# A GLA scan stage in which output buffers alternate through all heads, loads stand between the stores, and turned keys are copied behind the square

## What is computed

```python
g_f = (log_sigmoid(r_f @ w_af + b_af) / GATE_NORM).reshape(B, T, N_HEADS_GLA, HEAD_DK)
...
o_f, s_f = _gla_scan(q, k, v, g_f, s_f0)
o_b, s_b = _gla_scan(q[:, ::-1], k[:, ::-1], v[:, ::-1], g_b[:, ::-1], s_b0)
o = (o_f + o_b[:, ::-1]).astype(x.dtype)
o = _rmsnorm(o, gla_norm_g).reshape(B, T, GLA_VDIM) * jax.nn.silu(gate_a)
```

## Time and profile before

| | |
|---|---|
| median of 3 runs | 2041.45 us (2041.24 to 2043.97) |
| the profiled execution, its own time | 2043.08 us |
| its span in the trace | 2041.3 us |
| PE busy | 1946.9 us (95%) |
| PE weight loads | 1779.2 us (87%) |
| DVE busy | 997.1 us (49%) |
| ACT busy | 889.3 us (44%) |
| POOL busy | 576.2 us (28%) |
| mean granted TensorE clock | 0.982 |

### The profile page before, as it was taken

The page is one execution under the profiler, slowest core; times in us unless marked ns, Lnnn a source line. Parts: engine busy times, 40 slices in busy tenths (PEclk is TensorE's granted clock), DMA queues, the critical chain, the costliest instruction groups (busy, mean ns, idle before and its releaser), DMA issues.

```text
span 2041.3 us, 30175 instructions
## 1 busy us (share of the span) xinstructions
PE 1946.9 (95%) x10585; PEld 1779.2 (87%) x10585; DVE 997.1 (49%) x1854; ACT 889.3 (44%) x1905; POOL 576.2 (28%) x643
## 2 busy tenths in 40 slices
PE   7899999999999999999999988779899999999997
PEld 2899999999999999999999776667798888898886
DVE  4778887764444345444443244445566422333333
ACT  3565667744445574344553245556643100211222
POOL 0236652323433314333330000000931022331122
PEclk9899999999999999999999998889899999999999
DMA  6578888777878887778889583552356666654433
GB/s 272 199 261 300 282 283 320 285 253 226 283 262 274 292 292 237 243 259 267 280 273 350 187 332 141 204 217 86 123 217 226 216 213 210 228 194 169 143 123 124
DMA packets 165243, 476.90 MB, mean 234 GB/s; under 512 B 14512, under 2 KB 51818, under 8 KB 156396
## 3 DMA queue, kind: packets, MB, share of 16 engines
q1 hardware_dynamic: 151276, 424.70, 60.4%
q10 hardware_dynamic: 13824, 50.34, 6.2%
HBM read 310.34 MB, written 155.20 MB: 228 GB/s over the span
## 4 chain that ended last, share of the span: by engine, by line
PE 85%; DMA 6%; DVE 3%; ACT 2%; POOL 2%; issue 1%; SPq 1%; POOLq 0%; ACTq 0%; DVEq 0%
PE bank L2020 48%; PE bank L2319 10%; PE bank L2271 10%; PE bank L2284 5%; PE bank L2148 2%; DMA og_dram<-og 2%; PE bank L2213 1%; PE bank L2137 1%; DMA w_raw<-in_w_in 1%; PE bank L2115 1%; POOL h_lo L970 1%; DMA v_ld<-v_dram 1%; PE bank L2044 1%; DMA x_st<-in_x 1%; PE bank L2060 1%
## 5 line engine op out<-in xcount | busy, mean ns | idle before, releaser
L2020 PE MATMUL bank<-h_hi,w_op 128*128 128x384 f32 x4032 | 1054.7, 337 | 11.2 <-DVE h_lo L1517 6.0
L2020 PEld LDWEIGHTS bank<-h_hi,w_op 128*128 128x128 f32 x4032 | 732.2, 188 | 15.1 <-issue 15.1
L2020 PE MATMUL bank<-h_lo,w_op 128*128 128x384 f32 x2016 | 675.1, 335 | 0.0
L2020 PEld LDWEIGHTS bank<-h_lo,w_op 128*128 128x128 f32 x2016 | 379.8, 188 | 0.0
L1511 DVE TENSOR_TENSOR w_op<-w_raw,w_op 128x512 fp32r<-128x512 f32 x240 | 187.3, 781 | 126.2 <-ACT w_op L1143 122.4
L1143 ACT ACTIVATE w_op<-w_raw 128x512 fp32r<-128x512 f32 x240 | 150.2, 627 | 161.6 <-PE bank L2020 154.1
L995 POOL TENSOR_TENSOR decs<-decs,qk_s 128x192 f32<-128x192 f32 x192 | 122.1, 672 | 333.7 <-ACT decs L1217 333.5
L2319 PE MATMUL bank<-in_a,pwa 128*128 128x512 f32 (+1 forms) x960 | 197.3, 368 | 0.0
L2319 PEld LDWEIGHTS bank<-in_a,pwa 128*128 128x128 f32 x960 | 167.3, 189 | 30.0
L2271 PE MATMUL bank<-ow,me_hi 128*128 128x512 f32 x576 | 177.3, 389 | 0.0
L1566 DVE TENSOR_TENSOR outs<-bank,u 128x384 f32<-128x384 f32 x180 | 99.5, 553 | 118.8 <-PE bank L2020 117.9
(11 more groups left out here) (222 smaller groups left out, 2647.4 us busy)
## 6 DMA issues: line engine op xcount, KB each, us to landing
w_op<-wt_dram SPq DMA_DIRECT2D x192, 512.0 KB, 5.4
wt_dram<-w_op ACTq DMA_DIRECT2D x96, 512.0 KB, 4.4
w_raw<-in_w_in SPq DMA_DIRECT2D x48, 768.0 KB, 5.9
w_raw<-in_w_in SPq DMA_DIRECT2D x24, 1024.0 KB, 6.8
qk_dec<-decs SPq DMA_DIRECT2D x48, 384.0 KB, 6.6
mg_dram<-outs SPq DMA_DIRECT2D x24, 768.0 KB, 6.8
swap<-qk_s SPq DMA_DIRECT2D x48, 192.0 KB, 5.6
v_dram<-outs SPq DMA_DIRECT2D x24, 384.0 KB, 4.8
```

Source lines behind the costliest of these rows:

```text
L2020: ins = pe.matmul(bnk, w_op[slot][:, part, k, :], h[:, j, k, :], start=(first and k == 0 and part == 0 and h is h_hi), stop=(k == HK - 1 a ...
```

## The change

The edits, all in the scan stage:

1. `og` buffers are chosen by the running number of the block, `NB * head + b`, modulo 2; the waits of `gate` and the last waits of SP are counted to match.
2. `load_keys` no longer loads the queries. `load_queries(head + 1)` is issued behind the store of block 0, `load_gates(head + 1)` behind that of block 1, `load_first_values(head + 2)` behind that of block 2. The parts of u are loaded in two pairs, one ahead of and one behind the store of block 4 of head 2.
3. On ACT, the first `k_out` of a step (of term run + 1) is issued one step earlier, between the square and the Ln.

```diff
--- before.py
+++ after.py
@@ -748,12 +748,14 @@
                 else:
                     load_values(head, 0, LT - V_FIRST)
                     load_values(head, LT, NT)
-                load_queries(head)
 
             def load_queries(head):
                 n, d = head % 2, kept_way(head)
                 sp.dma_start(kk[n][:, 1 - d, :], qk_dec[4 + head, :, 1 - d]).then_inc(s_ql[n], 16)
                 sp.dma_start(qd[n][:, :, :], qk_dec[head]).then_inc(s_ql[n], 16)
+
+            def load_mixed(g):
+                sp.dma_start(uf[:, g, :], u_dram[g]).then_inc(s_big[g], 16)
 
             def load_gates(head):
                 sp.dma_start(ga_ld[head % 2][:, :, :], ga_dram[2 * head:2 * head + 2].rearrange("e p n -> p e n")
@@ -773,28 +775,31 @@
             sp.wait_ge(s_ql[0], 32)
             load_keys(1)
             load_first_values(1)
-            load_gates(1)
             sp.wait_ge(s_pu, NKEPT)
             store_state(0, kept_way(0))
             for head in range(HEADS):
                 for b in range(NB):
                     t0, n = head_tokens(head, b)
-                    if b == 3 and head + 2 < HEADS:
-                        sp.wait_ge(s_o, NT * head + V_FIRST)
-                        load_first_values(head + 2)
                     if b == NB - 1 and head + 2 <= HEADS:
                         sp.wait_ge(s_o, NT * head + NT)
                         if head + 2 < HEADS:
                             load_keys(head + 2)
                         else:
-                            for g in range(GROUPS):
-                                sp.dma_start(uf[:, g, :], u_dram[g]).then_inc(s_big[g], 16)
+                            load_mixed(0)
+                            load_mixed(1)
                     sp.wait_ge(s_gt, NT * head + BLOCKS[b][0] // P + n // P)
                     sp.dma_start(og_dram[2 * head:2 * head + 2, :, t0:t0 + n].rearrange("e p n -> p e n"),
-                                 og[:, b % 2, :, 0:n]).then_inc(s_ogst[b % 2], 16)
-                if head + 2 < HEADS:
-                    load_gates(head + 2)
-                elif head + 2 == HEADS:
+                                 og[:, (NB * head + b) % 2, :, 0:n]).then_inc(s_ogst[(NB * head + b) % 2], 16)
+                    if b == 0 and head + 1 < HEADS:
+                        load_queries(head + 1)
+                    if b == 1 and head + 1 < HEADS:
+                        load_gates(head + 1)
+                    if b == 2 and head + 2 < HEADS:
+                        sp.wait_ge(s_o, NT * head + V_FIRST)
+                        load_first_values(head + 2)
+                if head + 2 == HEADS:
+                    load_mixed(2)
+                    load_mixed(3)
                     sp.dma_start(tab_e_raw[:, :, :, :], io["tab_e"]).then_inc(s_tab_e, 16)
                 sp.wait_ge(s_pu, STEP_TERMS[NT * head + NT - 1].stop)
                 store_state(head, 1 - kept_way(head))
@@ -806,8 +811,8 @@
             for n in range(2):
                 sp.dma_start(tab_o_raw[:, n, :, :], io["tab_o"][:, n]).then_inc(s_tab_o, 16)
             sp.dma_start(tab_c[:, :], io["tab_c"]).then_inc(s_tab_o, 16)
-            sp.wait_ge(s_ogst[0], 16 * 3 * HEADS)
-            sp.wait_ge(s_ogst[1], 16 * 2 * HEADS)
+            for n in range(2):
+                sp.wait_ge(s_ogst[n], 16 * (NB * HEADS // 2))
             sp.wait_ge(s_fst, 16 * 2 * HEADS)
             for g in range(GROUPS - 1, -1, -1):
                 if g == 0:
@@ -1342,10 +1347,9 @@
                 k_out(g)
             act.wait_ge(s_ost[1], 16 * stored_before(LAST + 2))
             scale_queries(0)
+            k_out(run_term(0) + 1)
             for s in range(len(STEPS)):
-                run, others = run_term(s), kept_terms(s)
-                if run is not None:
-                    k_out(run + 1)
+                others = kept_terms(s)
                 if s + 1 < len(STEPS):
                     scale_queries(s + 1)
                 if others:
@@ -1357,6 +1361,8 @@
                 act.activation(junk2[:, :], o, ACT.Square, accum_out=rms[:, 0:1]).then_inc(s_sq2, 1)
                 for g in others[1:]:
                     k_out(g + 1)
+                if s + 1 < len(STEPS) and run_term(s + 1) is not None:
+                    k_out(run_term(s + 1) + 1)
                 act.wait_ge(s_sq2, s + 1)
                 act.activation(rms[:, 1:2], rms[:, 0:1], ACT.Ln, scale=1.0 / DV, bias=EPS).then_inc(s_ln2, 1)
                 act.wait_ge(s_ln2, s + 1)
@@ -1767,15 +1773,14 @@
             def gate(s):
                 head, x = STEPS[s]
                 n, b = head % 2, min(x // 4, NB - 1)
+                nth = NB * head + b
                 c = chunk_at(head, x)
                 at = c * P - head_tokens(head, b)[0]
-                if x == BLOCKS[b][0] // P:
-                    stored = (2 if b % 2 else 3) * head + b // 2
-                    if stored:
-                        dve.wait_ge(s_ogst[b % 2], 16 * stored)
+                if x == BLOCKS[b][0] // P and nth > 1:
+                    dve.wait_ge(s_ogst[nth % 2], 16 * (nth // 2))
                 dve.wait_ge(s_ot, s + 1)
                 for e in range(2):
-                    ins = dve.scalar_tensor_tensor(og[:, b % 2, e, at:at + P], bank[7][:, e * P:e * P + P],
+                    ins = dve.scalar_tensor_tensor(og[:, nth % 2, e, at:at + P], bank[7][:, e * P:e * P + P],
                                                    cols[:, C_GG + e:C_GG + e + 1], ga_ld[n][:, e, c * P:c * P + P],
                                                    ALU.mult, ALU.mult)
                 ins.then_inc(s_gt, 1)
```

## The result

The changed kernel took 1982.12 us (median of 4 runs, 1981.83 to 1984.80) against 2042.71 (2041.24 to 2044.45) for the kernel before on the same chip: a ratio of 0.9706, 95% interval 0.9689 to 0.9723. It is faster by 60.6 us, where the text above forecast 1979.5 in a range of 1974 to 1993. The profiled execution took 1982.17 us (forecast 1981.1), its span is 1980.3.

A forecast was written before the change was run, and what follows sets the result against it. Bound by PE's scan stage: `gate` waits for stores, a wait for values, slow clock, and a ring through ACT. 38.7 + 10.3 + 13.5 - 0.5 = 62.0 us off 2043.08 gives 1981.1, median 1979.5, range 1974 to 1993.

The forecast's parts named there:

- Buffers: Start of heads 1 to 3: alternating buffers remove three waits of `gate` for a store and the slow clock behind, 38.7 us.
- What was to be late next: Block 1 of the new head needs block 4's store, landing by 1288, needed about 1291: not late, by 3 us.
- Loads at the start: Head 0, step x = 4: earlier values of head 1 remove PE's wait, 10.3 us (7 to 10.7), 0.4 us of wait left.
- The higher landing time: Values at the start: by the skill's 358 GB/s, landing 15.0 us instead of 13.6, wait 1.5 us, total 1 us higher.
- The copy: Steps with a kept term: copy behind the square makes PE the bound, 4.5 us in each of three heads, 13.5 (0 to 14.4).
- The rival that the copy gains nothing: Kept-term steps: ACT's ring stays as long, as copy and Ln wait for PE's transpose; time 1993, chance 0.10 (nothing or little).
- the ring: Dependency loop of a kept-term step through PE and ACT; forecast 2.4 us with the change, below PE's 3.04.
- The slower rival: Every scan step: moved copy puts ACT behind PE, 4.3 us a step, about 2082 us in all; chance 0.02.
- Folds of u: POOL's last fold before the Fourier products: 13.0 us slack, 2.5 us left after the change, so 0 us.
- The rival: Folds of u become the bound: later POOL start uses up the 2.5 us margin, time 1980 to 1985; chance 0.04.
- The end of head 3: Scaling ahead of the Fourier products meets a longer POOL fold: -0.5 us, between +2.0 and -2.3.
- The median: Whole kernel: median of the runs 1.6 us below the profiled execution's 1981.1, so 1979.5 us.

The follow-up runs named there:

- e1: Kernel before with only the og buffers alternating through all heads; loads and copy as before: 2004.34 us, ratio 0.9815.
- e5: Changed kernel with the copy of turned keys put back, so new buffers and spread loads only: 1998.00 us, ratio 0.9781.
- e4: Kernel before with only the store of block 4 issued ahead of the loads at the end of heads 0 to 2: 2008.72 us, ratio 0.9839.
- e7: Changed kernel with the buffers put back, so spread loads and moved copy only: 1995.14 us, ratio 0.9766.
- e9: The changed kernel run once more, unaltered, in another job: 1985.43 us, ratio 0.9717 to the kernel before.
- e2: Kernel before with only the loads spread in SP's queue; buffers and copy as before: 2006.23 us, ratio 0.9825.
- e8: Changed kernel, first Fourier product not waiting for the last scaling of `fin`, last output turned two products later: 1981.89 us, ratio 0.9703.
- e10: The kernel of e8 run again, side by side with e9: 1981.55 us, ratio 0.9693 to the kernel before.

## Why the prediction was right

**The sum.** Scan stages give each term when the parts are added one after the other: 284.3 before, 246.9 with the buffers, 237.1 with the loads too, 221.4 with the copy. That is 37.5, 9.8 and 15.6 us, 62.9 in all; forecast were 38.7, 10.3 and 13.5, less 0.5. The scan also holds two pieces that differ from trace to trace beside the edits: the kept terms ahead of head 0, which took 16.90 us before, 17.66 in e1, 17.60 in e5 and 16.47 in the changed kernel (the two long ones at a lower clock), and the last scaling. Between the two, the parts give 39.7, 9.5 and 13.9 us.

**Buffers.** Right. In heads 1 and 2 (from keys L745 to keys L745, and from there to u) e1 is 14.0 and 14.1 us shorter than the kernel before, and from the issue of u to the last scaling 10.5: 38.6 for 38.7. The rest of the 39.7 fell in head 0, where e1 happened to wait 7.2 us for values and not 7.54, with a shorter slow stretch behind it. Of the 38.7 us, PE standing still was 31.6; the other 7 were the slow clock behind each stop. In heads 1 to 3 of e1 (1280 to 1434 us) the clock is 1.00. e4 adds what the text had only as the cause of the landing time: the place in the queue is enough. What was to be late next, block 1's `gate`, isn't. The values and the store of block 4 near the end of head 0 of the changed kernel (start, us, engine, line), then the same two with KB and us to landing:

```profile
1265.07 0.46 SPq L736 DMA_DIRECT2D v_ld<-v_dram  x1
1268.49 0.37 SPq L791 DMA_DIRECT2D og_dram<-og  x1
```
```profile
v_ld<-v_dram SPq DMA_DIRECT2D x1, 1152.0 KB, 9.0
og_dram<-og SPq DMA_DIRECT2D x1, 256.0 KB, 6.2
```

The store lands at 1268.49 + 6.2 = 1274.7, and the store of block 0, behind whose last `gate` block 1 begins, is issued only at 1279.48. The margin is over 4.8 us where I gave 3: I had put block 1 five steps behind the head's start, but `gate` runs later behind its step than I counted. An error on the safe side.

**Loads at the start.** Right. From the transpose at its start to the keys L745, head 0 took 67.73 us before and 57.15 in e5: 10.6 less, and with the copy 0.25 of wait comes back, so 10.3 as forecast (the 9.8 above is against e1, whose wait was the shorter one). The values of head 1 land 13.5 us after their issue (13.6 taken from the keys in their old place), and of the wait 0.25 us is left where I took 0.4 (3.84 us for this step, 3.59 for the next one):

```profile
1224.41 0.31 PE L2107 MATMUL bank<-consts,kk 128*128 128x128 f32 x1
1224.66 0.70 PE L2120 MATMUL bank<-v_ld,kin 128*128 128x256 f32 x2
```

A step with both kinds of product elsewhere has no such pause, and the clock of this stretch is 1.00 where it was 0.82. The higher landing time that I estimated by the Trainium skill ("DMA: Bandwidth & Descriptors", where 436 GB/s comes from) did not come: 13.5 us against its 15.0, and PE did not wait 1.5 us. That the last bit of wait was shorter than 0.4 us is luck, since the margin was put at none.

**The copy.** Right: 4.70 us in each of heads 1 and 2, where I took 4.5 of 4.8, and 4.5 in head 0 (57.15 to 52.62 us), with the 0.25 us of wait in it. That is 13.9 for 13.5; most of what I held back was not needed. The 15.6 us of the scan have 1.1 from the kept terms ahead of head 0 and 0.6 from the last scaling in them, which are not the copy's. The rival that the copy gains nothing had the ring at fault; with 0.28 us of ACT waiting for PE in place of PE waiting for ACT, it is PE that sets the step. The slower rival needed the next output product to wait for this step's copy, and it doesn't.

**Folds of u.** Right: no cost. In the changed kernel POOL's last fold ends at 1424.40 + 2.35 = 1426.75 and PE comes to it at 1429.83, a margin of 3.1 us (2.5 forecast):

```profile
1424.40 2.35 POOL L1035 TENSOR_TENSOR he<-he 128x1020 f32<-128x1020 f32 x1
...
1429.83 1.95 PE L2203 MATMUL bank<-cw,uf 128*128 128x128 f32 x16
```

The rival was real all the same: e4, which starts POOL a few us later, has 0.14 us of margin.

**The end of head 3.** Here sign and size came out (-0.64 us: L1760 took 2.98 us, L1754 2.34), but the range of +2.0 to -2.3 says how little of that was known: that it came out so close is luck. Over the traces this one instruction took from 1.08 us (e7) to 3.81 (e1), by where POOL's folds happened to stand. The rule of the Trainium skill ("SBUF — State Buffer", "Who interferes with whom") is borne out: L1760 ends at 1416.93 in the changed kernel, 0.15 us behind the fold's end at 1416.78, at 1416.75 in e9, 0.15 behind 1416.60, and so in every trace. Whole 4.5 us, which the rule would give had it just missed the fold's start, were not met. What I did not price is the clock: in six of the traces PE lost some 1.6 us besides.

**The median.** 1982.1 for 1979.5. In the profile 1.7 us of it stand ahead of the scan, where nothing was changed. I had subtracted 1.6 us, since the execution profiled before lay that much above its median; the changed kernel's lay at its own (1982.17 and 1982.12). A single execution carries an uncertainty of that size into the sum.

**Still open.** The profiled executions of e1 and e2 were 7.8 and 4.7 us above their medians, and in both the rest behind the folds is 2.4 to 2.6 us longer (547.1 and 546.9 for 544.5). No run tells why. The two profiled executions of the changed kernel are 2.8 us apart: 1.6 in the folds (the clock behind the gap), 1.4 in the rest, 0.6 in the scan, less 0.8 ahead of it. Whether the chip or the phase of POOL decides that was not separated. A like piece varies without any edit ahead of the steps: the kept terms took 16.34 us in e8 and 17.56 in e10, which are one kernel.

## What to carry to other kernels

When a buffer comes free by a store, read the queue and not the engine: the bytes issued ahead of that store set the wait. Moving the store ahead of the loads (e4), taking loads from in front of it (e2) and giving it another buffer (e1) each won 33 to 37 of 61 us here, and the two that ran together far less than their sum (e5: 44.7 for 72.9, some 10 of e2's being the start of head 0). So price such edits as substitutes, and give each one its own term only for what the others leave. In a ring through two engines, put the small copy that the other engine waits for ahead of the long operation that nobody waits for soon: 4.7 us in a stretch of 53. After a gain of this size, look for what used to be hidden in the stall: here a fold chain with 13 us to spare has 3, and a scaling of 0.35 us that waits for GpSimd is on the path.

## What the runs showed of the hardware that was not expected

- **One gap, two clocks.** At the same place of the same program PE idle for 2.29 us was followed by a clock of 1.00, and idle for 2.50 us by one of 0.57 over 3 us. The loss was 1.5 us on 64 small products, beside the gap itself. The kernel without the gap (e10) had runs within 1.7 us of each other.
- **Rate of one core.** In the folds of e4 the queues moved 426 to 430 GB/s over stretches of 3 us (1448 to 1457 us), above the 396 of the earlier trace rows, while the products ran at a clock of 1.00. The changed kernel reached 430 at the same place (1429 to 1432 us).
